# Stick-breaking attention on one core: scores and attended values in two passes in place of three

## What is computed

```python
def stick_breaking_mixer(h, w_qkv, w_o):          # 16 heads of 64
    q, k, v = jnp.split(h @ w_qkv, 3, axis=-1)
    return stick_breaking_attention(q, k, v) @ w_o

# for each head, query t and key s < t, z = q.k / 8:
#   log_keep = where(s < t, -softplus(z), 0)
#   log_a    = log_sigmoid(z) + sum of log_keep over the keys between s and t
#   out[t]   = sum over s < t of exp(log_a) * v[s]
```

## Time and profile before

| what | value |
| --- | --- |
| median of 3 runs | 1883.11 us (1882.21 to 1883.39) |
| the profiled execution, its own time | 1877.12 us |
| its span in the trace | 1875.4 us |
| mean granted TensorE clock | 0.995 of full speed |
| PE busy | 1841.6 us, 98% |
| DVE busy | 1426.8 us, 76% |
| ACT busy | 912.5 us, 49% |
| POOL busy | 503.8 us, 27% |

### The profile page before, as it was taken

One profiled execution on the slowest core, in us unless ns is written; L12 is line 12 of the kernel. 1 busy time (PEld: TensorE's weight loads), 2 busy tenths in 40 slices (PEclk: granted clock), 3 DMA queues, 4 the chain that ended last, 5 costly groups with the idle time before them and its releaser, 6 DMA issues.

```text
span 1875.4 us, 29435 instructions
## 1 busy us (share of the span) xinstructions
PE 1841.6 (98%) x11817; PEld 1647.8 (88%) x11817; DVE 1426.8 (76%) x1309; ACT 912.5 (49%) x1110; POOL 503.8 (27%) x379
## 2 busy tenths in 40 slices
PE   6999999999999999999999999999999999999998
PEld 6999988887789999888999998888888889999886
DVE  7898876589888879755889885654777688899753
ACT  6444543355275445444554453434655475455442
POOL 3344402200023443001344410221333223443021
PEclk8999999999999999999999999999999999999999
DMA  8788642232277786436778742222111277886321
GB/s 226 181 196 192 159 138 90 74 95 68 79 154 183 182 200 157 135 90 146 181 175 194 187 139 91 89 90 68 46 45 45 68 159 173 202 192 173 114 90 45
DMA packets 228251, 248.84 MB, mean 133 GB/s; under 512 B 7781, under 2 KB 196273, under 8 KB 227649
## 3 DMA queue, kind: packets, MB, share of 16 engines
q1 hardware_dynamic: 179232, 195.58, 34.0%
q0 software_dynamic: 48816, 51.98, 18.0%
q10 hardware_dynamic: 112, 0.03, 0.0%
HBM read 241.27 MB, written 2.10 MB: 130 GB/s over the span
## 4 chain that ended last, share of the span: by engine, by line
PE 78%; DVE 10%; ACT 4%; issue 3%; POOL 2%; DMA 2%; DVEq 0%; ACTq 0%; POOLq 0%
PE ps L604 34%; PE ps L400 13%; PE ps L401 13%; PE ps L402 13%; DVE w_lo L1541 3%; DVE y L1834 2%; DMA stage<-in_w_ffn_gate_dram 2%; PE ps L934 2%; POOL chain L2164 1%; PE ps L913 1%; PE ps L919 1%; ACT w_hi L1074 1%; DVE w_lo L1512 1%; PE ps L566 1%; ACT w_hi L1036 1%
## 5 line engine op out<-in xcount | busy, mean ns | idle before, releaser
L1541 DVE TENSOR_TENSOR w_lo<-stage,w_hi 128x1024 fp32r<-128x1024 f32 x264 | 435.5, 1662 | 19.4 <-ACT w_hi L1074 17.9
L604 PE MATMUL ps<-xs_hi,w_hi 128*128 128x256 f32 x2464 | 340.7, 280 | 10.7 <-ACT w_hi L1074 9.1
L604 PE MATMUL ps<-xs_lo,w_hi 128*128 128x256 f32 x2464 | 338.6, 279 | 2.6 <-DVE xs_lo L1752 1.9
L604 PE MATMUL ps<-xs_hi,w_lo 128*128 128x256 f32 x2464 | 338.7, 279 | 0.5 <-DVE w_lo L1541 0.2
L604 PEld LDWEIGHTS ps<-xs_hi,w_hi 128*128 128x128 f32 x2464 | 309.2, 189 | 13.5 <-issue 12.9
L604 PEld LDWEIGHTS ps<-xs_lo,w_hi 128*128 128x128 f32 x2464 | 308.8, 189 | 3.6 <-DVE xs_lo L1752 2.5
L604 PEld LDWEIGHTS ps<-xs_hi,w_lo 128*128 128x128 f32 x2464 | 308.6, 189 | 1.6 <-DVE w_lo L1541 1.5
L400 PE MATMUL ps<-xs_hi,w_hi 128*128 128x512 f32 x704 | 278.7, 396 | 0.7 <-issue 0.4
L401 PE MATMUL ps<-xs_lo,w_hi 128*128 128x512 f32 x704 | 278.2, 395 | 0.0
L402 PE MATMUL ps<-xs_hi,w_lo 128*128 128x512 f32 x704 | 278.2, 395 | 0.0
L1074 ACT ACTIVATE w_hi<-stage 128x1024 fp32r<-128x1024 f32 x176 | 181.3, 1055 | 161.5 <-DMA stage<-in_w_ffn_gate_dram 113.3
(11 more groups left out here) (240 smaller groups left out, 2705.0 us busy)
## 6 DMA issues: line engine op xcount, KB each, us to landing
stage<-in_w_ffn_up_dram SPq DMA_DIRECT2D x88, 512.0 KB, 4.1
stage<-in_w_ffn_gate_dram SPq DMA_DIRECT2D x88, 512.0 KB, 5.9
stage<-in_w_ffn_down_dram SPq DMA_DIRECT2D x88, 512.0 KB, 3.8
chain<-in_w_ffn_gate_dram POOLq DMA_DIRECT2D x47, 512.0 KB, 7.6
stage<-in_w_ffn_gate_dram POOLq DMA_DIRECT2D x44, 512.0 KB, 8.5
chain<-in_w_ffn_up_dram SPq DMA_DIRECT2D x43, 512.0 KB, 7.2
stage<-in_w_qkv_dram SPq DMA_DIRECT2D x24, 512.0 KB, 4.7
stage<-in_w_in_ab_dram SPq DMA_DIRECT2D x16, 512.0 KB, 4.6
```

The source lines that it names most:

```text
L604: mm = pe.matmul(ps[:, bank + BANK_OF[item], t * HS:(t + 1) * HS], w[:, slot, (2 * k + t) * P:(2 * k + t + 1) * P], xs[:, PART_OF[item], k ...
L1541: dve.tensor_tensor(w_lo[:, slot, :], src, w_hi[:, slot, :].bitcast(F32), ALU.subtract).then_inc(item_lo_made, 1)
```

## The change

- `qk_hi`, `qk_lo` become three tiles. `k_both` holds, for each head of a pair, `hi` of its k in the head's own 64 partitions and `lo` in the other 64. `q_both` holds, for each head, `hi` of its q in both halves. `q_lo` holds `lo` of q as before.
- `scores`: per key block one matmul over all 128 rows (k_hi q_hi + k_lo q_hi) and one over the head's 64 rows (k_hi q_lo). 8 matmuls in place of 12.
- `v_cat` replaces `v_hi` and `v_lo`: for each token block and head, 64 columns of `hi` and then 64 of `lo`. `attend` has two passes, over prob_hi and prob_lo, each with [v_hi, v_lo] of one head; half of the result rows come from `hi`, half from `lo`, and they have to be added.
- ACT: `split_proj` issues four copies of 64x512 for q and two for k, in place of one of 128x512. The copy to `o_att` is replaced by a copy of the other 64 rows of bank 7 into `sq`, counted in the new semaphore `o_moved`.
- DVE: `proj_low` issues two subtractions of 64x512 in place of one of 128x512. A new `add_o(h-2)` stands behind `prob_lo` in every turn: it adds 64 rows of bank 7 to `sq`, writes `o_att` and counts `o_copied`, which ACT had counted.
- `split_out`, `split_v`, `v_low` and `out_tile` use the new places. The product v_lo prob_lo is now in the sum as well.

```diff
@@ -178,8 +178,9 @@
             a_lo = sb("a_lo", [P, CT, S], F32R, conv_scope)
         with ExitStack() as att_scope:
             qk_f = sb("qk_f", [P, S], scope=att_scope)
-            qk_hi = sb("qk_hi", [P, 2, 2, S], F32R, att_scope)
-            qk_lo = sb("qk_lo", [P, 2, 2, S], F32R, att_scope)
+            q_both = sb("q_both", [P, 2, 2, S], F32R, att_scope)
+            q_lo = sb("q_lo", [P, 2, S], F32R, att_scope)
+            k_both = sb("k_both", [P, 2, 2, S], F32R, att_scope)
             prob = sb("prob", [P, SCORES], scope=att_scope)
             prob_hi = sb("prob_hi", [P, SCORES], F32R, att_scope)
             prob_lo = sb("prob_lo", [P, SCORES], F32R, att_scope)
...
@@ -187,8 +188,7 @@
             keep_hi = sb("keep_hi", [P, SCORES], F32R, att_scope)
             keep_lo = sb("keep_lo", [P, SCORES], F32R, att_scope)
             o_att = sb("o_att", [P, DT, S], scope=att_scope)
-            v_hi = sb("v_hi", [P, TT, D], F32R, att_scope)
-            v_lo = sb("v_lo", [P, TT, D], F32R, att_scope)
+            v_cat = sb("v_cat", [P, TT, HEADS, 2, DH], F32R, att_scope)
         mixer_scope.close()
         with ExitStack() as end:
             out_tok = sb("out_tok", [P, TT, D], scope=end)
...
@@ -390,6 +391,11 @@
             w = ffn_weights[n][0 if item in (T3, W22) else 1]
             odd = int(item in (W21, W22))
             return w.rearrange("(k two p) f -> p two k f", two=2, p=P)[:, odd, :, bass.ds(step.count(2 * P, 0), 2 * P)]
+
+        def o_split(j):
+
+            both = v_cat[:, :, 2 * j:2 * j + 2].rearrange("p t h a c -> p t (h a c)")
+            return both[:, :, 0:P], both[:, :, P:2 * P]
 
         def rows_of(w, k0, k1, cols):
 
...
@@ -897,11 +903,11 @@
                 elif h == 0:
                     pe.wait_ge(v_lo_made, 2 * TT)
                 for b in range(TT):
-                    r = slice(r0, r0 + DH)
-
-                    mm = three(pe, zcols(h, b), qk_hi[r, j % 2, 1, b * P:(b + 1) * P],
-                               qk_lo[r, j % 2, 1, b * P:(b + 1) * P], qk_hi[r, j % 2, 0, b * P:S],
-                               qk_lo[r, j % 2, 0, b * P:S], start=(b < 3))
+                    r, keys = slice(r0, r0 + DH), slice(b * P, (b + 1) * P)
+                    pe.matmul(zcols(h, b), k_both[:, j % 2, h % 2, keys], q_both[:, j % 2, h % 2, b * P:S],
+                              start=(b < 3), stop=False, skip_group_check=True)
+                    mm = pe.matmul(zcols(h, b), k_both[r, j % 2, h % 2, keys], q_lo[r, j % 2, b * P:S],
+                                   start=False, stop=False, skip_group_check=True)
                 mm.then_inc(scores_summed, 1)
 
             def suffix(h):
...
@@ -923,17 +929,16 @@
 
             def attend(h):
 
-                j = h // 2
                 pe.wait_ge(prob_hi_made, h + 1)
                 if h >= 1:
                     pe.wait_ge(o_copied, h)
-                for n, (v, part) in enumerate(((v_hi, prob_hi), (v_lo, prob_hi), (v_hi, prob_lo))):
-                    if n == 2:
+                for n, part in enumerate((prob_hi, prob_lo)):
+                    if n == 1:
                         pe.wait_ge(prob_lo_made, h + 1)
                     for b in range(TT):
-                        mm = pe.matmul(ps[:, 7, b * P:S], v[:, b, j * P:(j + 1) * P],
+                        mm = pe.matmul(ps[:, 7, b * P:S], v_cat[:, b, h].rearrange("p a c -> p (a c)"),
                                        part[:, KEY_OFF[b]:KEY_OFF[b] + KEY_COLS[b]], start=(n == 0 and b == 0),
-                                       stop=(n == 2 and b == TT - 1), skip_group_check=True)
+                                       stop=(n == 1 and b == TT - 1), skip_group_check=True)
                 mm.then_inc(att_summed, 1)
 
             def out_tile(q, bank, k_from=0, k_to=4):
...
@@ -942,9 +947,8 @@
                 pe.wait_ge(w_lo_made, c0 + 13 + n)
                 for k in range(k_from, k_to):
                     pe.wait_ge(o_lo_made, k0 + k + 1)
-                    cols = slice((k0 + k) * P, (k0 + k + 1) * P)
                     mm = three(pe, ps[:, bank, :].rearrange("p (t c) -> p t c", t=TT), *tile(n % 2, 4 * k + q % 4),
-                               v_hi[:, :, cols], v_lo[:, :, cols], start=(k == 0), stop=(k == 3))
+                               *o_split(k0 + k), start=(k == 0), stop=(k == 3))
                 if k_to < 4:
                     return
                 if q % 4 == 3:
...
@@ -1428,12 +1432,17 @@
                 act.wait_ge(tok_rinv_made, 2)
                 act.wait_ge(w_used, c0 + 3 + 2 * half)
                 for t in range(TT):
-                    act.activation(v_hi[:, t, half * 512:(half + 1) * 512], ps[:, 4 - 4 * half + t, :], ACT.Copy,
-                                   scale=tok_rinv[:, t:t + 1]).then_inc(v_hi_made, 1)
+                    act.activation(v_cat[:, t, 8 * half:8 * half + 8, 0], ps[:, 4 - 4 * half + t, :].rearrange("p (h c) -> p h c", h=8),
+                                   ACT.Copy, scale=tok_rinv[:, t:t + 1]).then_inc(v_hi_made, 1)
 
             def split_proj(n):
                 act.wait_ge(proj_scaled, n + 1)
-                act.activation(qk_hi[:, (n // 2) % 2, n % 2, :], qk_f[:, :], ACT.Copy).then_inc(proj_hi_made, 1)
+                to = (k_both if n % 2 else q_both)[:, (n // 2) % 2]
+                if n % 2 == 0:
+                    act.activation(to[DH:P, 0, :], qk_f[0:DH, :], ACT.Copy)
+                    act.activation(to[0:DH, 1, :], qk_f[DH:P, :], ACT.Copy)
+                act.activation(to[0:DH, 0, :], qk_f[0:DH, :], ACT.Copy)
+                act.activation(to[DH:P, 1, :], qk_f[DH:P, :], ACT.Copy).then_inc(proj_hi_made, 1)
 
             def zall(h):
                 at = 3 * (h % 2) * 512
...
@@ -1442,8 +1451,7 @@
             def split_out(j):
 
                 act.wait_ge(o_copied, 2 * j + 2)
-                act.activation(v_hi[:, :, j * P:(j + 1) * P], o_att[:, j, :].rearrange("p (t c) -> p t c", t=TT),
-                               ACT.Copy).then_inc(o_hi_made, 1)
+                act.activation(o_split(j)[0], o_att[:, j, :].rearrange("p (t c) -> p t c", t=TT), ACT.Copy).then_inc(o_hi_made, 1)
 
             split_proj(0)
             split_proj(1)
...
@@ -1473,8 +1481,8 @@
                     split_proj(h + 2)
                 if h >= 2:
                     act.wait_ge(att_summed, h - 1)
-                    r = slice(DH * (h % 2), DH * (h % 2) + DH)
-                    act.activation(o_att[r, (h - 2) // 2, :], ps[r, 7, :], ACT.Copy).then_inc(o_copied, 1)
+                    r, other = slice(DH * (h % 2), DH * (h % 2) + DH), slice(DH - DH * (h % 2), P - DH * (h % 2))
+                    act.activation(sq[r, :], ps[other, 7, :], ACT.Copy).then_inc(o_moved, 1)
                 if h >= 3 and h % 2:
                     split_out((h - 3) // 2)
                 if h % 2 and h <= 13:
...
@@ -1989,9 +1997,9 @@
             def v_low(half):
                 for t in range(TT):
                     dve.wait_ge(v_hi_made, 4 * half + t + 1)
-                    cols = slice(half * 512, (half + 1) * 512)
-                    dve.scalar_tensor_tensor(v_lo[:, t, cols], ps[:, 4 - 4 * half + t, :], tok_rinv[:, t:t + 1],
-                                             v_hi[:, t, cols].bitcast(F32), ALU.mult,
+                    heads = slice(8 * half, 8 * half + 8)
+                    dve.scalar_tensor_tensor(v_cat[:, t, heads, 1], ps[:, 4 - 4 * half + t, :].rearrange("p (h c) -> p h c", h=8),
+                                             tok_rinv[:, t:t + 1], v_cat[:, t, heads, 0].bitcast(F32), ALU.mult,
                                              ALU.subtract).then_inc(v_lo_made, 1)
 
             def scale_proj(n):
...
@@ -2008,8 +2016,11 @@
             def proj_low(n):
                 dve.wait_ge(proj_scaled, n + 1)
                 dve.wait_ge(proj_hi_made, n + 1)
-                dve.tensor_tensor(qk_lo[:, (n // 2) % 2, n % 2, :], qk_f[:, :],
-                                  qk_hi[:, (n // 2) % 2, n % 2, :].bitcast(F32), ALU.subtract).then_inc(proj_lo_made, 1)
+                for e, (r, other) in enumerate(((slice(0, DH), slice(DH, P)), (slice(DH, P), slice(0, DH)))):
+                    hi = (k_both if n % 2 else q_both)[r, (n // 2) % 2, e, :].bitcast(F32)
+                    to = k_both[other, (n // 2) % 2, e, :] if n % 2 else q_lo[r, (n // 2) % 2, :]
+                    ins = dve.tensor_tensor(to, qk_f[r, :], hi, ALU.subtract)
+                ins.then_inc(proj_lo_made, 1)
                 dve.wait_ge(proj_lo_made, n + 1)
 
             def zall(h):
...
@@ -2018,9 +2029,15 @@
 
             def split_out(j):
                 dve.wait_ge(o_hi_made, j + 1)
-                cols = slice(j * P, (j + 1) * P)
-                dve.tensor_tensor(v_lo[:, :, cols], o_att[:, j, :].rearrange("p (t c) -> p t c", t=TT),
-                                  v_hi[:, :, cols].bitcast(F32), ALU.subtract).then_inc(o_lo_made, 1)
+                o_hi, o_lo = o_split(j)
```

(11 more changed lines are left out.)

## The result

The changed kernel takes 1909.77 us (median of 4 runs, 1903.23 to 1918.28) against 1882.66 (4 runs, 1877.34 to 1883.39): ratio 1.0154, interval 1.0121 to 1.0187, 27 us slower. The direction was forecast, the size not: 1897.2 with a range up to 1904. The profiled execution took 1903.23 us, 26.1 more than that of before.

The account below looks back on a forecast made before the run. PE was taken to bound the kernel before, a loop of ACT and DVE waits the changed one. Hand-kept tables gave +14.1 us at the last output tile, added to the median 1883.11: 1897.2 us, range 1889 to 1904.

Parts of the forecast that it names:

- the ring: Loop of waits through ACT and DVE, closed at split_out by add_o: 26.05 us for two heads against PE's 23.85.
- The signs in mid-attention: Expected in the later profile: PE idle some 2 us for two heads, every second head 26 us apart.
- A change of shape: PE switching between 128-row and 64-row matmuls in scores: 0.14 us each, bounds 0 and 0.19, seven inside the scores.
- PE's turn: PE's time per head: 12.42 less 0.64 for attended values plus 0.15 for scores, giving 11.93 us.
- The third rival: Dearer changes of shape on PE: +16.6 us at 0.25 each, about +20 at 0.3; chance 0.10.
- the fourth: Rival: changes of shape on PE free, scores gain in full, ACT-DVE wait loop stays: +12.1 us; chance 0.05.
- The first heads: Heads 0 to 5: PE still leads, as the first split_out comes in turn 3; scores(5) starts 0.5 us earlier.
- The tail: Last heads: PE idles 5.6 us before the first output tile, then 2.8; +12.1 at scores(15).
- The sum: Whole attention stage laid out by hand-kept tables: +14.1 us at the last output tile.
- Rivals 1 and 2: Cheaper 64-row pieces on ACT and DVE: either PE stays the bound, -7 us, chance 0.07; or +2.5 us, chance 0.06.

Follow-up runs that it names:

- e2: Changed kernel with DVE's add_o moved from behind prob_lo to before prob_hi; ratio 1.0067 to the kernel before, stage +12.5 us.
- e3: Changed kernel with split_out of a pair moved one turn later on ACT and DVE, last pair staying; ratio 1.0077 to the kernel before, stage +11.9 us.
- e1: Changed kernel with the scores grouped, four 128-row matmuls and then four 64-row ones; ratio 1.0127 to the kernel before, stage +23.7 us.
- e5: Kernel before with only the scores half of the change, attended values as before; ratio 1.0082 to the kernel before, stage +10.9 us.
- e9: Kernel before with only the scores half, every scores matmul over 128 rows by zero filling; ratio 0.9966 to the kernel before, stage -5.6 us.
- e6: Changed kernel with scores, split_proj and proj_low of the kernel before, so the attend half alone; ratio 1.0072 to the kernel before, stage +9.6 us.
- e10: Both halves, zero-filled scores, split_out later, scale_proj(h+3) then add_o before prob_hi, q-doubling copies behind the sq copy; 1875.78 us against 1886.64, ratio 0.9943.
- e7: Attend half alone with split_out one turn later and scale_proj(h+3) before prob_hi; ratio 0.9961 to the kernel before, stage -7.5 us.
- e11: The kernel of e7 measured once more; 1879.78 us against 1886.64 for the kernel before, ratio 0.9967.
- e12: Changed kernel with split_out one turn later and scale_proj(h+3) before prob_hi, scores still alternating; ratio 1.0054 to the kernel before, stage +8.7 us.

## Why the prediction was right in kind and wrong in size

**What failed.** The time lies above the stated range. The largest miss is the length of the ring, 26.05 us in the prediction and 27.25 in the trace, mostly because the copies and subtractions of 64 rows were priced too low; it makes 5.1 of the 12.2 us that are missing in the stage. The second is a step that the prediction does not have at all: behind several of PE's idles the clock fell, which cost some 3.1 us behind the output tiles' waits and 1.3 in turn 1. The third is turn 1 itself, where the prediction had PE leading.

**The ring: right.** ACT's row before `split_out` shows 6.8 us of idle ended by `add_o`; e2 and e3 take the wait away in two ways and give back 13.8 and 14.3 us of stage; e1 shows that PE was not in it. Its length was under-sized, and every term lies in the rows above:

| piece of the ring | forecast | measured |
| --- | --- | --- |
| `split_out`, weights | 2.40 | 2.35 |
| activations and exp, even head | 4.88 | 4.98 |
| four copies of q, to DVE | 2.28 | 2.66 |
| `proj_low` | 1.33 | 1.42 |
| `keep_hi`, `keep_lo` | 2.40 | 2.45 |
| activations and exp, odd head | 4.88 | 4.87 |
| two copies of k, to DVE | 1.24 | 1.36 |
| `proj_low` | 1.33 | 1.51 |
| `keep` and `prob` split | 4.56 | 4.92 |
| `add_o`, to ACT | 0.75 | 0.73 |
| sum | 26.05 | 27.25 |

The copies of 64 rows start 0.64 us apart, not 0.52: I had taken the distance from a place where two copies begin at the same partition (1366.44 to 1366.96 in the earlier trace rows), while here each reads from another half of the partitions than its neighbour. The kernel before has the longer distance too, in every odd turn, where the copy to `o_att` begins at partition 64:

```profile
1354.03 0.62 ACT L1436 ACTIVATE qk_hi<-qk_f 128x512 fp32r<-128x512 f32 x1
1354.68 0.60 ACT L1477 ACTIVATE o_att<-ps 64x512 f32<-64x512 f32 x1
```

They are 0.65 us apart, so the price was to be had beforehand. On DVE the same shows as 0.10 more behind `prob_lo`. And 0.27 of the splits comes from DVE's wait for POOL's stretched masks. Over the four pairs from head 5 to head 13 the forecast was +4.9, measured +10.0 (109.31 against 99.34): 1.2 to 1.3 a pair more.

The signs in mid-attention were a distance of 26 us for two heads and 2.2 us of idle on PE. The distances are 29.3 and 25.5 in turn, 27.3 on average, with 1.2 to 1.4 us of idle on PE in the long ones and 0.7 in the short ones: in the long ones the idle was followed by a low clock (granted 0.88 over the pair), and PE was busy with slower matmuls in place of idling.

**A change of shape: right, but 0.175 and not 0.14.** The upper bound of 0.19 was the better reading of the same rows. The sum also counts seven changes where eight lie between the first matmul of the scores and the suffix: at 0.14 it should have been 2.34 us, not 2.20, and eight at 0.175 give the 2.6 measured. PE's turn became 12.27, not 11.93. The third rival's price of 0.25 was too high, and the fourth, changes for free, falls with e5 and e9. The Trainium skill (TensorEngine Tiling (Array Packing), "Tiling Modes") has the rule that a change of mode drains the engine; the trace agrees in so far as every change costs 0.175 us, and does not show the drain itself.

**The first heads: wrong.** I had PE leading by 0.5 us at scores(5); it was behind by 2.4. Turn 0 gave 0.49 of that and turn 1 2.37, and the next three turns took back 0.15 each. PE in turn 1, and the clock there:

```profile
1296.73 0.85 PE L919 MATMUL ps<-keep_hi,neg_tri 128*128 128x512 f32 x3 [0.56 <-DVE keep_hi L2077]
...
1300.91 0.54 PE L406 MATMUL ps<-xg_hi,w_hi 128*128 128x512 f32 x1
```

```profile
1295.00:1300.00 5.00, 4.44 (x19) 3.69 (x19) 3.72 (x5) 1.68 (x2) 0.00 (x0) 0.77 0.00 0
```

Dearer scores make 0.49 of the 2.37. PE idled 0.56 us for `keep_hi`, which stands on DVE behind `proj_low` and so behind the four copies of q. The suffix behind that idle took 4.18 us where the kernel before has 2.91: 1.3 more, at a low clock. ACT's first activation also waited 3.97 us for `keep_lo` there. In e6, without these copies and with the scores of before, scores(2) stands 10.81 us behind scores(1), as in the kernel before; here it is 13.19.

**The tail: right in place, too small in size.** The forecast idle before the first output tile was 5.6 us, measured 5.82. But the tiles behind it ran at a low clock: from scores(13) to scores(15) 36.97 us, 11.8 over before, where I had 7.7. The waits were nearly as forecast (5.82 and 2.83, against 5.6 and 2.8). The two tiles behind them took 4.53 and 4.19 us in place of 2.90, and `attend` behind the second 0.2 more: 3.1 us, most of the 4.1 that are missing. That an idle of PE costs a second time, by the clock, was in no term of my sum. In mid-attention the same drops (granted 0.50 from 1350 to 1355 us and from 1405 to 1410) cost nothing, since `split_out` came at its 27.24 us all the same.

**The sum.** At the last output tile +26.3 against +14.1: 2.9 from the first heads, 5.1 from the ring's length, 4.1 from the last heads up to scores(15), nearly nothing behind it. Missing altogether were the clock and the idle of turn 1; nearly all the other terms erred to the same side. Varying each by itself, as I did for the range, gave 13 to 18. The range should have added the misses. No rival gave the measured time either; the nearest, the third, had +20 with changes of shape at 0.3, for a reason that the trace does not bear out.

**Rivals 1 and 2** fell: pieces of 64 rows cost as much as whole ones.

## What to carry to other kernels

When the producer of a semaphore moves to another engine, look where in that engine's list it stands and what is queued behind the wait on the consumer's: one add behind the last big piece of DVE's turn made ACT's next head late, and moving it by two instructions gave back 14 us of the stage. Here a matmul with 64 contraction rows between full ones cost more than a full one: filling the rows with zeros took the scores from 2.63 to 1.23 us. With both, and the small copies out of the way, the idea of the change is worth 11 us (e10), and its attend half alone 5 to 7 (e7, e11).

## What the runs showed of the hardware that was not expected

- An idle of 3.3 us on PE was followed by some 5 us at a granted clock of 0.50, with PE busy all the time (e3); in e12, with the idle gone, the clock was 1.00 in the same place. Much shorter idles were followed by a low clock too: 0.56 us in turn 1 and 1.19 us at 1347.34 in the changed kernel. Not every one was: behind 0.54 us in the same turn of e3 the granted clock stayed at 1.00.
- ACT's copies of 64x512 lie 0.63 to 0.65 us apart when neighbours begin at different partitions with what they read from SBUF or with what they write, and 0.54 where the second writes to the same partitions as the first and reads PSUM (1381.65 to 1382.19). What exactly sets the difference was not tried.
- POOL's four masks took 1.03 us while DVE idled and 3.83 while it ran its casts and subtractions. In the kernel before the same masks took 1.6 and 2.9, so this was there to be seen, though not on a path then.
